# Down projection of a hybrid encoder layer by one level of Strassen's scheme (one core)

## What is computed

```python
def conv_ffn(u, w_up, conv_w, conv_b, w_down):
    h = u @ w_up                                   # 512 x 1024 by 1024 x 5632
    h = lax.conv_general_dilated(h, conv_w[:, None, :], ...) + conv_b   # 3 taps along the tokens
    gate, up = jnp.split(h, 2, axis=-1)
    return (jax.nn.gelu(gate, approximate=True) * up) @ w_down          # 512 x 2816 by 2816 x 1024
...
    h = h + rmsnorm(conv_ffn(u, ...), g_post_ffn[i])
```

## Time and profile before

| | us |
|---|---|
| median of 3 runs | 876.66 (876.43 to 876.73) |
| the profiled execution's own time | 877.14 |
| its span, first to last instruction | 875.4 |
| PE busy | 864.4 (99%) |
| DVE, ACT, POOL busy | 412.0, 402.2, 455.8 |

### The profile page before, as it was taken

The page is one execution under the profiler, slowest core; times in us unless marked ns, Lnnn a source line. Parts: engine busy times, 40 slices in busy tenths (PEclk is TensorE's granted clock), DMA queues, the critical chain, the costliest instruction groups (busy, mean ns, idle before and its releaser), DMA issues.

```text
span 875.4 us, 13103 instructions
## 1 busy us (share of the span) xinstructions
PE 864.4 (99%) x4248; PEld 726.8 (83%) x4248; DVE 412.0 (47%) x877; ACT 402.2 (46%) x716; POOL 455.8 (52%) x630
## 2 busy tenths in 40 slices
PE   8999999999999999999999999999999999999997
PEld 7888887888888888888888798888888888888885
DVE  5677877888766732222231555444444444200004
ACT  5566666877666643323232535444444444311112
POOL 4554443334344457665666838555555555555551
PEclk9999999999999999999999999999999999999999
DMA  6541232322232223333237314333333332322202
GB/s 214 155 124 53 81 88 67 94 75 76 79 79 78 66 80 101 100 88 105 87 120 241 96 49 121 96 96 96 96 96 96 96 96 96 122 97 96 99 21 96
DMA packets 131998, 85.60 MB, mean 98 GB/s; under 512 B 6807, under 2 KB 121439, under 8 KB 131956
## 3 DMA queue, kind: packets, MB, share of 16 engines
q1 hardware_dynamic: 130906, 81.34, 30.9%
q10 hardware_dynamic: 1050, 3.72, 1.2%
HBM read 82.89 MB, written 2.14 MB: 97 GB/s over the span
## 4 chain that ended last, share of the span: by engine, by line
PE 95%; DVE 1%; POOL 1%; DMA 1%; ACT 1%; issue 1%; SPq 0%; DVEq 0%; POOLq 0%; ACTq 0%
PE banks L1353 29%; PE banks L1355 28%; PE banks L1354 28%; PE banks L1524 2%; PE banks L1433 2%; PE banks L1432 2%; PE banks L1496 1%; DMA ring_raw<-in_w_in_dram 1%; PE banks L1503 1%; PE banks L1487 1%; DVE scratch L1277 1%; POOL pages L574 1%; PE banks L1444 0%; PE banks L1372 0%; DVE u_lo L982 0%
## 5 line engine op out<-in xcount | busy, mean ns | idle before, releaser
L566 POOL TENSOR_TENSOR ring_lo<-ring_raw,ring_hi 128x256 fp32r<-128x256 f32 x560 | 419.7, 781 | 371.5 <-ACT ring_hi L680 371.4
L1353 PE MATMUL banks<-u_hi,ring_hi 128*128 128x512 f32 (+1 forms) x768 | 300.5, 391 | 0.5 <-DVE u_lo L982 0.5
L1355 PE MATMUL banks<-u_hi,ring_lo 128*128 128x512 f32 (+1 forms) x768 | 296.1, 386 | 0.0
L1354 PE MATMUL banks<-u_lo,ring_hi 128*128 128x512 f32 (+1 forms) x768 | 295.6, 385 | 0.0
L680 ACT CAST ring_hi<-ring_raw 128x1024 fp32r<-128x1024 f32 x140 | 145.9, 1044 | 138.3 <-PE banks L1355 130.0
L1355 PEld LDWEIGHTS banks<-u_hi,ring_lo 128*128 128x128 f32 x768 | 144.3, 188 | 29.3
L1353 PEld LDWEIGHTS banks<-u_hi,ring_hi 128*128 128x128 f32 x768 | 144.4, 188 | 28.0 <-DVE u_lo L982 0.7
L1354 PEld LDWEIGHTS banks<-u_lo,ring_hi 128*128 128x128 f32 x768 | 144.5, 188 | 27.3
L1318 DVE SCALAR_TENSOR_TENSOR wide<-banks,cols,wide 128x511 f32<-128x511 f32 x88 | 66.0, 750 | 102.2 <-ACT wide L935 96.1
L1353 PE MATMUL banks<-ring_hi,pages 128*128 128x512 f32 x240 | 93.9, 391 | 0.1
L1354 PE MATMUL banks<-ring_lo,pages 128*128 128x512 f32 x240 | 93.4, 389 | 0.0
(11 more groups left out here) (143 smaller groups left out, 1001.9 us busy)
## 6 DMA issues: line engine op xcount, KB each, us to landing
ring_raw<-in_w_ffn_up_dram SPq DMA_DIRECT2D x88, 256.0 KB, 3.1
ring_raw<-in_w_in_dram SPq DMA_DIRECT2D x60, 256.0 KB, 3.4
ring_raw<-in_w_gate_dram SPq DMA_DIRECT2D x48, 256.0 KB, 3.1
ring_raw<-in_w_ffn_down_dram SPq DMA_DIRECT2D x44, 256.0 KB, 2.8
ring_raw<-in_w_out_dram SPq DMA_DIRECT2D x16, 256.0 KB, 2.8
scratch<-in_x_dram SPq DMA_DIRECT2D x4, 512.0 KB, 6.3
ring_raw<-in_w_proj_a_dram SPq DMA_DIRECT2D x8, 256.0 KB, 2.7
ring_raw<-in_w_proj_c_dram SPq DMA_DIRECT2D x8, 256.0 KB, 3.1
```

The lines of the kernel that those rows point to most:

```text
L566: last = pool.tensor_tensor(wlo[:, r, c], raw[:, r, c], whi[:, r, c].bitcast(F32), ALU.subtract)
L1353: pe.matmul(out, lhs_hi, rhs_hi, start=start, stop=False)
L1354: pe.matmul(out, lhs_hi, rhs_lo, start=False, stop=False)
L1355: return pe.matmul(out, lhs_lo, rhs_hi, start=False, stop=stop)
```

## The change

The operands are cut in halves: tokens 0 to 255 and 256 to 511, channel blocks 0 to 10 and 11 to 21 (FH = 11), output columns 0 to 511 and 512 to 1023. With A11, A21 (first channels, early and late tokens), A12, A22 (second channels) and B11, B12, B21, B22 for the weights, Winograd's form of Strassen's scheme is used:

- DVE makes S1 = A21 + A22, S3 = A11 - A21, S2 = S1 - A11, S4 = A12 - S2 of the activations (`token_sums`), and T3 = B22 - B12, T1 = B12 - B11, T2 = T3 + B11, T4 = B21 - T2 of the weights.
- Pass 1 (k = 0 to 10): M1 = A11 B11 in banks 0 and 2, M5 = S1 T1 in 1 and 3, M7 = S3 T3 in 4 and 6, M6 = S2 T2 in 5 and 7.
- Between the passes the banks are edited in place: ACT copies M1 out, DVE adds M6, M7 and M5 (`keep_u2`, `make_e21`, `add_m5`), ACT writes one sum back into the banks of M7.
- Pass 2 (m = 0 to 10) goes on accumulating into the edited banks: M2 = A12 B21 onto banks 0 and 2, M4 = A22 T4 onto 4 and 6, M3 = S4 B22 onto 1 and 3.

Each product has, per k, two token tiles and three matmuls. The up loop now runs over pairs of channel blocks (i, i + 11). A12, A22 and S4 of ten pairs are stored to DRAM and read back in pass 2; the residual tokens are stored to DRAM as well, since their pages hold the T2 parts. Weight parts lie in four buffers: two made of the ring, two of `u_hi` and `u_lo`, which are free only after the up projection. Raw weights use three slots, and a fourth in two halves for B22. Per k of pass 1 the low part of B11 is made by POOL (two pieces of 128 x 256), those of T1, T3 and T2 by DVE; in pass 2 that of B22 by POOL and those of B21, T4 and the activations by DVE. The gain of the final norm is loaded late by SP, and the tiles of the tail come in the order 0, 2, 3, 1.

The core of the diff, with indentation reduced and blank lines left out:

```diff
-ACT_HI, ACT_LO = 0, FT
 EARLY_PG = 6
+FH = FT // 2
+PASS2_PG = (0, 3, 6, 9)
+JUNK_PG = 12
+LAST_PAIR_AT = 6
+DOWN_SLOTS = (2, 3, 0)
+DOWN_ORDER = (0, 2, 3, 1)
+BY_TILE, BY_PRODUCT = 4, 3
...
+def store_second(i):
+    sp.wait_ge(act_sums, 4 * i + 4)
+    sp.dma_start(act2_dram[i], second_raw).then_inc(act2_stored, 16)
...
+def load_down(n):
+    if n < 3:
+        ring_free(B_DOWN + n)
+    elif n < FH + 3:
+        sp.wait_ge(b11_lo, n - 2)
+        sp.wait_ge(t1_lo, n - 2)
+    else:
+        sp.wait_ge(b21_lo, n - FH - 2)
+        sp.wait_ge(b22_lo, n - FH - 2)
+    for dst, c in zip(down_raw(n), (slice(0, 512), slice(512, 1024))):
+        sp.dma_start(dst, down_v[:, n, c]).then_inc(down_loaded[n % 3], 16)
+def load_half(n):
+    if n < 2:
+        ring_free(B_DOWN + 3)
+    else:
+        sp.wait_ge(t3_lo, n - 1)
+    sp.dma_start(half_raw(n), down_v[:, FH + n, 512:1024]).then_inc(half_loaded[n % 2], 16)
+for n in range(3):
+    load_down(n)
+load_half(0)
+load_half(1)
+store_second(FH - 2)
+def load_second(m):
+    if m == 0:
+        sp.wait_ge(act2_stored, 16 * (FH - 1))
+        sp.wait_ge(h_stored, 16 * TT)
+    if m >= 2:
+        sp.wait_ge(act2_lo, m - 1)
+    sp.dma_start(second_again(m), act2_dram[m]).then_inc(act2_loaded[m % 2], 16)
+for n in range(2, FH):
+    load_half(n)
+    load_down(n + 1)
...
+for n in range(FH + 1, FT):
+    load_down(n)
+    if n - FH + 1 < FH - 1:
+        load_second(n - FH + 1)
+    if n == FT - 2:
+        sp.wait_ge(t4_lo, 7)
+        for t in (0, 1):
+            sp.dma_start(x_tok[:, t, :], h_dram[t]).then_inc(h_again[t], 16)
+        sp.dma_start(g_post_2, g_post_ffn[0].partition_broadcast(P)).then_inc(gain_ffn_loaded, 16)
+sp.wait_ge(act2_lo, FH - 1)
+for t in (2, 3):
+    sp.dma_start(x_tok[:, t, :], h_dram[t]).then_inc(h_again[t], 16)
...
+def in_halves(lo, src, hi):
+    for c in (slice(0, 256), slice(256, 512)):
+        last = pool.tensor_tensor(lo[:, c], src[:, c], hi[:, c].bitcast(F32), ALU.subtract)
+    return last
+for n in range(FH):
+    pool.wait_ge(down_hi, 4 * n + 1)
+    hi, lo = down_part(n, 0)
+    in_halves(lo, down_raw(n)[0], hi).then_inc(b11_lo, 1)
+for m in range(FH):
+    hi, lo = down_part(FH + m, 1)
+    pool.wait_ge(down2_hi, 3 * m + 1)
...
+def split_tokens(i):
+    act.wait_ge(act_sums, i * 4 + 2)
+    act.copy(pages[:, i * 4, :], first_tokens).then_inc(act_hi, 1)
...
+def split_first(n):
+    buffer_free(n)
+    act.wait_ge(down_loaded[n % 3], 32 * (n // 3 + 1))
+    act.copy(down_part(n, 0)[0], down_raw(n)[0]).then_inc(down_hi, 1)
+    act.wait_ge(t_sums, 3 * n + 2)
+    act.copy(down_part(n, 1)[0], down_raw(n)[1]).then_inc(down_hi, 1)
+    act.copy(down_part(n, 3)[0], half_raw(n)).then_inc(down_hi, 1)
+    act.wait_ge(t_sums, 3 * n + 3)
+    act.copy(down_part(n, 2)[0], t2_page(n)).then_inc(down_hi, 1)
+def split_second(m):
+    n = FH + m
+    buffer_free(n)
+    act.wait_ge(down_loaded[n % 3], 32 * (n // 3 + 1))
+    act.copy(down_buffer(n)[0][:, 0:1024], raw[:, DOWN_SLOTS[n % 3], :]).then_inc(down2_hi, 1)
+    act.wait_ge(t4_sums, m + 1)
+    act.copy(down_part(n, 2)[0], t2_page(m)).then_inc(down2_hi, 1)
+    if m < FH - 1:
+        act.wait_ge(act2_loaded[m % 2], 16 * (m // 2 + 1))
+    act.copy(pass2_parts(m)[0], second_again(m)).then_inc(down2_hi, 1)
...
+for n in range(1, FH):
+    split_first(n)
+    if n == LAST_PAIR_AT:
+        split_tokens(FH - 1)
+split_second(0)
+act.wait_ge(m1_done, 1)
+act.wait_ge(t3_lo, FH)
+for t in range(2):
+    act.copy(kept_part(t), psum[:, M1_BANKS[t], :]).then_inc(m1_copied, 1)
+for t, src in enumerate((spare_part, kept_part(0))):
+    act.wait_ge(e21_done, t + 1)
+    act.copy(psum[:, M7_BANKS[t], :], src).then_inc(e21_back, 1)
+for m in range(1, FH):
+    split_second(m)
...
+def token_sums(i):
+    dve.wait_ge(conv, i * 10 + 10)
+    dve.tensor_tensor(s1, a21, a22, ALU.add).then_inc(act_sums, 1)
+    dve.tensor_tensor(a21, a11, a21, sub).then_inc(act_sums, 1)
+    dve.wait_ge(act_sums, i * 4 + 1)
+    dve.tensor_tensor(s2, s1, a11, sub).then_inc(act_sums, 1)
+    dve.wait_ge(act_sums, i * 4 + 3)
+    dve.tensor_tensor(s4, a12, s2, sub).then_inc(act_sums, 1)
+    for part, src in enumerate((first_tokens, mixed_sums)):
+        dve.wait_ge(act_hi, i * 2 + (part + 1))
+        dve.tensor_tensor(pages[:, i * 4 + (2 * part + 1), :], src,
+                          pages[:, i * 4 + 2 * part, :].bitcast(F32), sub).then_inc(act_lo, 1)
...
+def split_first(n):
+    b11, b12 = down_raw(n)
+    b22 = half_raw(n)
+    buffer_free(n)
+    dve.wait_ge(down_loaded[n % 3], 32 * (n // 3 + 1))
+    dve.wait_ge(half_loaded[n % 2], 16 * (n // 2 + 1))
+    dve.tensor_tensor(b22, b22, b12, sub).then_inc(t_sums, 1)
+    dve.tensor_tensor(b12, b12, b11, sub).then_inc(t_sums, 1)
+    dve.wait_ge(t_sums, 3 * n + 1)
+    dve.tensor_tensor(t2_page(n), b22, b11, ALU.add).then_inc(t_sums, 1)
+    dve.wait_ge(down_hi, 4 * n + 2)
+    hi, lo = down_part(n, 1)
+    dve.tensor_tensor(lo, b12, hi.bitcast(F32), sub).then_inc(t1_lo, 1)
+    dve.wait_ge(down_hi, 4 * n + 3)
+    hi, lo = down_part(n, 3)
+    dve.tensor_tensor(lo, b22, hi.bitcast(F32), sub).then_inc(t3_lo, 1)
+    dve.wait_ge(down_hi, 4 * n + 4)
+    hi, lo = down_part(n, 2)
+    dve.tensor_tensor(lo, t2_page(n), hi.bitcast(F32), sub).then_inc(t2_lo, 1)
+def split_second(m):
+    n = FH + m
+    b21 = down_raw(n)[0]
+    t4 = t2_page(m)
+    buffer_free(n)
+    dve.wait_ge(down_loaded[n % 3], 32 * (n // 3 + 1))
+    dve.tensor_tensor(t4, b21, t4, sub).then_inc(t4_sums, 1)
+    dve.wait_ge(down2_hi, 3 * m + 1)
+    hi, lo = down_part(n, 0)
+    dve.tensor_tensor(lo, b21, hi.bitcast(F32), sub).then_inc(b21_lo, 1)
+    dve.wait_ge(down2_hi, 3 * m + 2)
+    hi, lo = down_part(n, 2)
+    dve.tensor_tensor(lo, t4, hi.bitcast(F32), sub).then_inc(t4_lo, 1)
+    dve.wait_ge(down2_hi, 3 * m + 3)
+    hi, lo = pass2_parts(m)
+    dve.tensor_tensor(lo, second_again(m), hi.bitcast(F32), sub).then_inc(act2_lo, 1)
+ffn_taps(2 * FH - 2, FH - 1, 0)
+ffn_product(2 * FH - 2, 0, first_tokens)
+dve.wait_ge(h_stored, 16 * TT)
+split_first(0)
+ffn_taps(2 * FH - 1, FH - 1, 1)
+split_first(1)
+dve.wait_ge(act2_stored, 16 * (FH - 1))
+ffn_product(2 * FH - 1, 1, second_raw[:, 0:512])
+for n in range(2, FH):
+    split_first(n)
+    if n == LAST_PAIR_AT:
+        token_sums(FH - 1)
+split_second(0)
+def keep_u2(t):
+    dve.wait_ge(m1_copied, t + 1)
+    dve.tensor_tensor(kept_part(t), psum[:, M6_BANKS[t], :], kept_part(t), ALU.add).then_inc(u2_done, 1)
+def make_e21(t, dst):
+    dve.wait_ge(u2_done, t + 1)
+    dve.tensor_tensor(dst, psum[:, M7_BANKS[t], :], kept_part(t), ALU.add).then_inc(e21_done, 1)
+def add_m5(t, e21):
+    dve.wait_ge(e21_done, t + 1)
+    dve.tensor_tensor(psum[:, M6_BANKS[t], :], psum[:, M5_BANKS[t], :], e21, ALU.add).then_inc(c22_done, 1)
+    dve.tensor_tensor(psum[:, M5_BANKS[t], :], psum[:, M5_BANKS[t], :], kept_part(t), ALU.add)\
+       .then_inc(e12_done, 1)
+dve.wait_ge(m6_done, 1)
+keep_u2(0)
+keep_u2(1)
+dve.wait_ge(m7_done, 1)
+make_e21(0, spare_part)
+dve.wait_ge(m5_first, 1)
+add_m5(0, spare_part)
+dve.wait_ge(e12_done, 1)
+make_e21(1, kept_part(0))
+split_second(1)
+dve.wait_ge(down_used, FH)
+add_m5(1, kept_part(0))
+for m in range(2, FH):
+    split_second(m)
...
-for k in range(FT - RING):
-    pe.wait_ge(w_lo_done, B_DOWN + k + 1)
-    pe.wait_ge(act_lo, k + 1)
-    for t in (2, 3, 0, 1):
-        if k == 0 and t == 0:
-            pe.wait_ge(conv, 5 * FT - 1)
-        for half in range(2):
-            mm = down_step(k, t, half)
-    mm.then_inc(tile_used, 1)
-pe.wait_ge(act_lo, FT)
-for t in range(TT - 1):
-    for k in range(FT - RING, FT):
-        pe.wait_ge(w_lo_done, B_DOWN + k + 1)
-        for half in range(2):
...
+def m1(k, t):
+    return product(M1_BANKS[t], t, mixed_tokens(k, 0), down_part(k, 0), k == 0, k == FH - 1)
...
+def m2(m, t):
+    return product_onto(M1_BANKS[t], t, second_tokens(m, 0), down_part(FH + m, 0))
...
+for k in range(1, FH - BY_PRODUCT):
+    first_ready(k)
+    for ready, make in ((b11_lo, m1), (t1_lo, m5), (t3_lo, m7), (t2_lo, m6)):
+        pe.wait_ge(ready, k + 1)
+        for t in range(2):
+            mm = make(k, t)
+    mm.then_inc(down_used, 1)
+late = range(FH - BY_PRODUCT, FH)
+for ready, make, done in ((b11_lo, m1, m1_done), (t2_lo, m6, m6_done), (t3_lo, m7, m7_done)):
+    for k in late:
+        if make is m1:
+            first_ready(k)
+        pe.wait_ge(ready, k + 1)
+        for t in range(2):
+            mm = make(k, t)
+    mm.then_inc(done, 1)
+pe.wait_ge(t1_lo, FH)
+for k in late:
+    mm = m5(k, 0)
+mm.then_inc(m5_first, 1)
+for k in late:
+    m5(k, 1).then_inc(down_used, 1)
...
+pe.wait_ge(m1_copied, 2)
+for m in range(2):
+    second_ready(m)
+    by_pair(m, m2)
+    if m == 0:
+        pe.wait_ge(e21_back, 2)
+    by_pair(m, m4)
+pe.wait_ge(e12_done, 2)
+for m in range(2):
+    by_pair(m, m3).then_inc(down_used, 1)
+for m in range(2, FH - BY_TILE):
+    second_ready(m)
+    by_pair(m, m2)
```

(18 more changed lines are left out.)

284 lines of the change are left out of this document (204 added, 80 removed).

## The result

| | before | after |
|---|---|---|
| median of 4 runs, us | 876.67 (876.43 to 876.73) | 889.02 (887.70 to 890.21) |
| profiled execution, us | 877.14 | 890.21 |
| its span, us | 875.4 | 888.4 |
| mean granted TensorE clock | 0.998 | 0.984 |
| matmuls of the down projection | 528 | 462 |

The ratio of the runs is 1.0142, with a 95% interval of 1.0129 to 1.0155: slower by 1.4%. The forecast was 886.3 us in a range of 870 to 898.

A forecast was written before the change was run, and what follows sets the result against it. PE, busy 99% of the span, was taken as the bound. 877.14 - 15.6 + 5.4 (pass 1) + 2.4 (bank edits) + 15.3 (pass 2) + 2.1 (clock) = 886.7 us profiled, 886.3 by the median; range 870 to 898.

The forecast's parts named there:

- What is removed: Down projection on PE: 66 fewer matmuls and 0.6 us of short waits, a gain of 15.6 us, leaving 104.7 us.
- an up projection that pays nothing: Up projection: the added sums and splits on DVE and ACT fit beside PE's 21.8 us per pair and cost nothing.
- One operation and the group of pass 1: DVE in pass 1: 0.62 us per operation alone, 4.85 us a group with POOL's pieces; PE loses 5.4 us.
- 0.47: Us that a DVE operation with two SBUF inputs was taken to lose to a POOL piece beside it.
- a price of the full 0.70: Rival: each POOL piece costs DVE 0.70 us, 4.6 us more in pass 1; within a case of chance 0.15.
- The bank edits: Between the passes: the split of m = 1 is ready 5.1 us after pass 1; PE loses 2.4 us.
- The group of pass 2: DVE's splits in pass 2: 4.55 us a group, bounds 4.1 to 5.4; eight groups from m = 2 take 36.5 us.
- the loop over SP's queue: Pass 2: weights of m queue behind a token read waiting for m - 2; two groups take 9.05 us.
- the 2 us of the forecast: End of pass 2: extra time for m = 10, whose weights stand behind three loads of 512 KB.
- The rival in which the waits stay small: POOL's pieces fall into DVE's gaps or POOL gives way: pass 2 groups 3.3 to 3.9 us, 864 to 874 us; chance 0.18.
- The clock: PE's clock falls in the last block, perhaps at M1 of k = 10 too; 2.1 us taken, at one place.
- The sum by steps: Down stage: pass 1 ends at 65.3 us, m = 2 is ready 9.7 later, the last split ends at 113.5.

The follow-up runs named there:

- e11: The changed kernel with POOL making each low part in one piece of 512 columns in place of two of 256; 888.51 us.
- e3: The changed kernel with SP's second-pass weight loads ahead of the token reads and the three tail loads behind the last weight load; 879.21 us.
- e8: The changed kernel with only weight loads and second-token reads reordered on SP's queue, the three tail loads left in place; 882.41 us.
- e12: e6 plus zero matmuls in two waits, a last block of three k-parts, and m = 10 asked for six matmuls later in it; 867.46 us.
- e1: The changed kernel with the last block of pass 2 taking two k-parts in place of four; 884.34 us.
- e7: The changed kernel with POOL computing 16 of 256 columns in each low-part piece, so nearly all that work is left out; 876.55 us.
- e6: The changed kernel with e3's queue order, one gathered k-part in pass 1, and a last block of two k-parts; 869.15 us.
- e5: The changed kernel with e3's queue order and one gathered k-part in pass 1, last block still of four k-parts; 873.85 us.
- e4: The changed kernel with TensorE multiplying by a matrix of zeros during its waits in both passes; 884.69 us.
- e2: The changed kernel with pass 1's products gathered over one last k-part in place of three; 883.54 us.

## Why the prediction held, step by step

The sign and the mechanism were right; 889.02 is 2.7 us over the forecast.

**What is removed: right.** 104.8 us of matmuls at full clock, as said, and an up projection that pays nothing.

**One operation and the group of pass 1: right.** 4.87 us a group for 4.85; DVE ended pass 1 at 54.2 us from the stage's start for 55.2; the waits in pass 1 were 4.9 for 5.4. The loss beside POOL was 0.54 us an operation, not 0.47. What I had wrong is how to read the earlier trace rows beside the Trainium skill. The Trainium skill, SBUF — State Buffer, section "SBUF: two separate sides", says that whoever starts first keeps the shared pair for its whole instruction. I set that rule against the 0.47 as if it meant a price of the full 0.70. e11 shows that they agree: the engine that comes second waits for the rest of the other's instruction, 0.54 us at 256 columns, 1.09 at 512, since it starts 0.2 later. By these runs the price depends on who started how much earlier, and my forecast took nearly the right size for it from a row.

**The bank edits: right.** 2.5 us for 2.4; the split of m = 1 was ready 5.1 us after pass 1's end, as predicted.

**The group of pass 2: right in size and in cause.** 4.55 us for 4.55, set by the loop over SP's queue: e3 and e8 take the loop away, and the group is 3.76 us. Behind m = 8 more was lost than the 2 us of the forecast: m = 9 was late as well, 2.8 us for both beyond the usual distance, and the stretch from m = 2 on took 1.9 us longer than summed. The weights of m = 9 landed 6.5 us after their issue, with the three loads issued right behind them; that these slowed them is likely but not shown apart. The rival in which the waits stay small named 3.3 to 3.9 us a group and 864 to 874 us, on the ground that POOL's pieces fall into DVE's gaps or POOL gives way. That did not happen: the two still meet twice a group. e3's group of 3.76 us and e12's 867.5 lie within its numbers, but by another way, the order of the loads and of the last block.

**The clock: mis-sized, and this is the step that failed.** "I take 2.1 [...] at one place." It fell at three, for 7.9 us of slow matmuls, of which about 5 lay on the path: 2.9 in pass 1 and 2.2 behind the last split. The sum by steps, from the stage's start: pass 1 ended at 67.7 for 65.3 (+2.9 of clock, -0.5 of wait), m = 2 was ready 0.5 sooner behind it, the eight groups took 1.9 longer, and the end came 0.2 later: 133.96 for 129.9 us, of which the up projection gave back 0.6. I had named M1 of k = 10 as a place where the clock might fall, and priced it at nothing. A fall there is not local: it moved the edits and every split queued behind them. The Trainium skill, TensorE: Matmul & The Clock Gate, section "What's actually happening", tells of a return after sustained work. By the rows, the clock was still at 0.50 after 5.6 us of steady matmuls behind the wait for k = 10 (799.8 to 805.4) and after 4.4 us behind the last split, and full soon after; in other executions it was back sooner (a loss of 1.5 us in place of 2.9 at the first place in e1, and in e7 and e11 1.5 in place of 2.1 at the second). No row of the kernel before could give such a length. The 2.1 us were the time in which the clock fell after PE's end, put in for the price of a low clock; that the place behind the last split cost 2.2 is luck.

## What to carry to other kernels

- When a scheme saves matmuls and adds work on another engine, follow that engine's chain to its last product and count the matmuls that are still to come. The length of TensorE's last block decided nearly 5 us here (e1, and e6 against e5), with the longer tail counted in; a block that asks for its last operands first turns every late operand into an idle TensorE.
- On one in-order DMA queue, a load that waits for the end of a group holds every load behind it. Put the one with the oldest condition first, and loads for the tail behind everything that the main loop wants.
- A wait on TensorE can cost more than its length: behind most of the waits of 2.5 us and more the slow matmuls cost another 1.5 to 2.9 us where work went on, behind those of 1.4 to 1.9 us nothing. Where the wait can't be closed, other work in it is worth the most where a chain hangs on what follows.

## What the runs showed of the hardware that was not expected

- Matmuls by a matrix of zeros keep TensorE at full clock: 1.00 in all stretches of e4, with waits of up to 5.5 us filled.
- How TensorE stood before the clock fell varies. Of twelve waits of 2.5 to 3.0 us in these traces nine were followed by matmuls at 0.50, within 1.4 us of their start, and three were not. In two of these three (e1 at 859.64, e11 at 852.92) TensorE did three matmuls and stood again, and the clock fell 1.2 us after their start, inside that next wait; in the third (e2 at 816.04) it stayed up. Of the waits of 1.4 to 1.9 us none was followed by slow matmuls before the next wait.
- DVE (with two inputs in SBUF) and POOL take turns: beside POOL pieces of 256 and 512 columns a DVE operation of 0.68 us takes 1.22 and 1.77. A pair of POOL pieces with 16 columns still takes 0.99 us on POOL but costs DVE about 0.02 us each (e7).
- A weight load of 256 KB landed in 3.5 us (median of 55) where it took 2.8 before, with 146 GB/s on average in the stage for 87. With the loads issued earlier (e3) nobody waited for it.
